# A two-part transformer kernel on one core: the second block's mixer, latent attention and tail made into one semaphore stage

## The chip, the cores and the metric

The kernel runs on one core of a Trainium2 chip. A core has five engines that run side by side, each with its own instruction queue: PE (TensorE, matrix multiply), DVE (VectorE), ACT (ScalarE), POOL (GpSimd) and SP (SyncE, which here only issues DMAs). They meet through semaphores. The metric is the device time of one execution in microseconds (us).

## The reference, cut to what matters

Two blocks of two layers each work on 512 positions of width 1024. The change is in the second block. One of its layers is

```python
u = rms_norm(x, g_mix) @ w_in
y_a = silu(layer_norm(depthwise_conv(a * sigmoid(gate))))            # conformer group
y_b = rms_norm(hgrn2(u_b), onorm) * silu(g)                           # recurrent group
y_c = gb * depthwise_conv(gc * xin)
y_d = mla(u_d)                                                        # latent attention, 4 heads
cat = rms_norm(concat(y_a, y_b, y_c, y_d) in 4 groups, g_branch)
x = x + cat @ w_out
mn = rms_norm(mem, g_mem)                                             # 256 rows of memory
q, k, v = rms_norm(rms_norm(x) @ x_wq), rms_norm(mn @ x_wk), mn @ x_wv
x = x + attention(q, k, v) @ x_wo
x = x + swiglu(rms_norm(x)) @ f_w2
```

## The kernel before

Everything is float32 and kept transposed: a tensor of width 1024 is 8 tiles of 128 partitions x 512 positions. A product with a weight tile is three float32r matmuls (`product`, L390 to L392) from a high and a low half of each operand. Weight tiles come by DMA (L358), ACT copies the high half (L367), POOL subtracts for the low half (L376).

A layer of the second block is three `nc.Block()`s, one after the other, each with one written-out instruction list per engine:

- **The mixer** (`second_mixer`): projections, the convolutions, the recurrent scan, queries and keys of the latent attention. At its end ACT takes a root for each head's key (`key_root(h)`: a Ln, L2052, then an Exp, L2054, of a sum that PE makes at L1904), squares the recurrent group (L2066) and the centred conformer group (L2073) into the buffer `PT`, and, after PE has summed those squares (L1940, L1943), takes three Ln (L2083 twice, L2085). The Exp that finishes each of these three roots is done by ACT at the start of the next block (L2337).
- **The latent attention** (`second_attention`, through `attention` and `attention_work`): 16 units (4 heads x 4 query blocks of 128). For unit n: PE scores (L743), DVE maximum and negation (L841, L844), ACT exponential (L805), DVE reciprocal (L854), POOL scaling (L880), PE transposes (L751) and ACT copies the result to `PT` (L814) four units later; after 8 units PE multiplies by the values (L757). The functions `side_act`, `side_dve`, `side_pool` put other work between the units by step number: the norm of the memory (ACT squares L529, DVE L523, L533, L540), two products that finish the conformer group (DVE L2361, steps 3 and 4), two for the recurrent group (DVE L2365, steps 5 and 6; POOL L2380, steps 8 and 10), three weight tiles. ACT and DVE follow each other closely: unit n's exponential waits for DVE's negation of n, and DVE's reciprocal of n, which stands in its list after the negation of n + 1, waits for that exponential.
- **The tail** (`second_tail`): PE sums the squares of each of the four groups of `cat` (`group_sum`, L2454), sums the memory's squares (L545), makes two key tiles of the memory (`key_tile`), then the output projection, cross attention and feed-forward.

Each of the three ends with `sem.stage_end()`, an all-engine barrier that also clears the stage's semaphores (L337):

```python
    def stage_end(self):
        numbers = sorted(s.num for s in self.numbers)
        assert numbers == list(range(numbers[0], numbers[-1] + 1))
        self.nc.all_engine_barrier(sems_to_clear=range(numbers[0], numbers[-1] + 1))
        self.stage = {}
```

The range that is cleared is that of every stage semaphore made so far: 13 at the first stage end, 76 from the second block's first mixer on. Leaving a `with nc.Block()` also writes an all-engine barrier of its own, without a clear (its rows carry the line of the `with`: L1771 for the mixer, L889 for the attention, L2438 for the tail).

Of the kernel before, what the change touches and what calls it, by code (L numbers as in the profile page):

```python
# [316 lines left out]
class Semaphores:  # L317


    def __init__(self, nc):  # L320
        self.nc, self.stream, self.stage, self.numbers = nc, {}, {}, []
# [3 lines left out]
    def __call__(self, name):  # L325
        if name in self.stream:
            return self.stream[name]
        if name not in self.stage:
            if len(self.stage) == len(self.numbers):
                self.numbers.append(self.nc.alloc_semaphore(f"stage_{len(self.numbers)}"))  # L330
            self.stage[name] = self.numbers[len(self.stage)]
        return self.stage[name]

    def stage_end(self):
# [3 lines left out]
        self.stage = {}  # L338
# [253 lines left out]
def build(nc, x_in, w1, small1, const_in, p_in, w2, small2, masks_in, mem_in, pos_in, out):  # L592
# [109 lines left out]
    def attention_work(*kinds, side_act=None, side_dve=None, side_pool=None, side_pe=None):  # L702
# [33 lines left out]
        def run_pe(pe):  # L736
            def scores(n):
                a, h, g, i = units[n]
                for m in range(a["maps"]):
                    s = first[n] + m  # L740
                    if s >= 4:
                        pe.wait_ge(sem("max_ready" if biased else "exp_done"), s - 3)
                    pe.matmul(banks[s % 4][:, 0:width(n)], a["q"](h, m, i), a["k"](h, m, width(n)), start=True,  # L743
                              stop=True).then_inc(sem("scored"), 1)

            def turn(n):
                pe.wait_ge(sem("prob_ready"), n + 1)
                if n >= 2:
                    pe.wait_ge(sem("pt_ready"), n - 1)
                for j in range(width(n) // P):  # L750
# [135 lines left out]
    def attention(weights, prefetch, work, before=None, first_act=None):  # L886

        run_pe, run_act, run_dve, run_pool = work
        with nc.Block() as block:  # L889
# [17 lines left out]
            def _(dve):  # L907
                run_dve(dve)

            @block.gpsimd  # L910
            def _(pool):
                run_pool(pool)
        sem.stage_end()
# [788 lines left out]
    B_R, DEVIATION, KEY_R = 36, 44, (45, 46, 47, 38)  # L1702
    NL = len(LEVELS)
    PAD = 15

    def second_mixer(layer, weights, prep):

        base = DEPTH * FIRST_TILES + layer * SECOND_TILES
# [62 lines left out]
        with nc.Block() as block:  # L1771
# [6 lines left out]
            def _(pe):  # L1778
# [55 lines left out]
                def scan_values(c):  # L1834
# [6 lines left out]
                    if c == 2:  # L1841
                        pe.wait_ge(sem("latent_log"), 2)
# [28 lines left out]
                pe.wait_ge(sem("kr_gained"), 1)  # L1871
# [27 lines left out]
                def key_sum(h):  # L1899
                    pe.wait_ge(sem("kr_square"), 4)  # L1900
                    pe.wait_ge(sem("key_square"), h + 1)
                    if h >= 2:
                        pe.wait_ge(sem("key_log"), h - 1)
# [874 lines left out]
```

## Time and profile before

| | |
|---|---|
| Time, median of 3 runs | 3219.67 us (3214.8 to 3219.79) |
| The profiled execution's own time | 3216.99 us |
| Its span (first to last instruction) | 3215.2 us |
| PE busy, share of the span | 95% |
| ACT / DVE / POOL busy | 41% / 50% / 49% |
| Mean granted TensorE clock | 0.984 of 2.4 GHz |

The profiled execution's time is 1.8 us more than its span. In the first layer of the second block the latent attention stands between 1903.2 and 1952.3 us of the span, in the second between 2674.2 and 2723.5. The profile names engines as above; PEld is the weight load of PE, and a `q` behind a name (ACTq) is that engine's sequencer, which runs waits, drains and barriers. PEclk is the granted TensorE clock: 1.00 is 2.4 GHz, 0.50 is 1.2 GHz.

### The profile page before, as it was taken

The page shows a single profiled execution, that of the slowest core. Times are in us where ns is not written, and L with a number is a line of the kernel's source. Part 1 is how long each engine was busy: PE and PEld are TensorE (multiplying, and loading weights), DVE is VectorE, ACT ScalarE, POOL GpSimd, SP SyncE. Part 2 cuts the span into 40 slices and gives each one's busy share as a digit, 9 for nine tenths or more (in the row PEclk, how much of TensorE's full clock was granted, in tenths as well). Part 3 has the DMA queues.
Part 4 walks back from the last instruction along what each step waited for, and adds up shares of the span by engine and source line. Part 5 has one row for each costly group of instructions (what it writes and reads, how often), then busy time and mean ns, then how long its engine had stood idle before and what let it go on. Part 6 is the DMA issues. An engine that isn't in the chain of part 4 may idle for free. (4 is left out here: it accounts for less than half of the span.)

```text
span 3215.2 us, 38320 instructions
## 1 busy us (share of the span) xinstructions
PE 3066.1 (95%) x14320; PEld 2394.0 (74%) x14320; DVE 1623.4 (50%) x2468; ACT 1327.0 (41%) x2194; POOL 1581.0 (49%) x862
## 2 busy tenths in 40 slices
PE   8989999999998999999999988899999988989999
PEld 6766788888766678888887756688888764768887
DVE  3863357732467434775348764433324955543321
ACT  4445433333443554333343475532323257442221
POOL 5634655554764455555565443344444534344443
PEclk9999999999999999999999989999999998999999
DMA  4211233333221123333323102233333211223333
GB/s 135 67 59 47 79 101 96 98 106 105 92 69 60 52 67 99 98 99 108 105 87 97 48 20 66 60 98 99 98 104 100 67 34 33 72 73 98 99 99 105
DMA packets 73736, 265.07 MB, mean 82 GB/s; under 512 B 8656, under 2 KB 9168, under 8 KB 73168
## 3 DMA queue, kind: packets, MB, share of 16 engines
q1 hardware_dynamic: 73552, 262.62, 26.6%
q8 instruction: 115, 1.88, 0.2%
q14 instruction: 69, 0.57, 0.1%
HBM read 260.49 MB, written 2.10 MB: 82 GB/s over the span
## 5 line engine op out<-in xcount | busy, mean ns | idle before, releaser
L376 POOL TENSOR_TENSOR low<-raw,high 128x1024 fp32r<-128x1024 f32 x482 | 1179.7, 2449 | 1148.8 <-ACT high L367 1115.5
L391 PE MATMUL bank<-slot_r,low 128*128 128x512 f32 (+1 forms) x3648 | 1423.8, 390 | 0.0
L392 PE MATMUL bank<-slot_r,high 128*128 128x512 f32 (+1 forms) x3648 | 1423.4, 390 | 0.0
L390 PE MATMUL bank<-slot_r,high 128*128 128x512 f32 (+1 forms) x3328 | 1323.8, 398 | 44.2 <-POOL low L376 15.0
L367 ACT ACTIVATE high<-raw 128x1024 fp32r<-128x1024 f32 x482 | 507.5, 1055 | 900.4 <-PE bank L392 826.7
L392 PEld LDWEIGHTS bank<-slot_r,high 128*128 128x128 f32 x3648 | 688.6, 189 | 147.2
L391 PEld LDWEIGHTS bank<-slot_r,low 128*128 128x128 f32 x3648 | 689.7, 189 | 144.5 <-issue 5.8
L390 PEld LDWEIGHTS bank<-slot_r,high 128*128 128x128 f32 x3328 | 629.0, 189 | 214.8 <-issue 50.3
L1624 DVE SCALAR_TENSOR_TENSOR tmp<-padded,small,tmp 128x512 f32<-128x512 f32 x176 | 209.7, 1249 | 0.0
L880 POOL TENSOR_SCALAR tmp<-tmp,stat 128x512 f32<-128x512 f32 (+3 forms) x128 | 79.9, 625 | 144.9 <-DVE stat L854 119.7
L2111 DVE SCALAR_TENSOR_TENSOR slots<-padded,small,slots 128x512 f32<-128x512 f32 x128 | 132.9, 1096 | 0.0
L1615 DVE TENSOR_TENSOR padded<-bank,rs 128x512 f32<-128x512 f32 x88 | 60.3, 686 | 138.9 <-PE bank L392 129.2
L2707 DVE TENSOR_TENSOR tmp<-bank,rs 128x512 f32<-128x512 f32 x44 | 30.4, 692 | 192.0 <-PE bank L392 186.8
L533 DVE SCALAR_TENSOR_TENSOR slot_r<-slots,small,slot_r 128x512 fp32r<-128x512 f32 (+1 forms) x80 | 93.5, 1168 | 44.0 <-ACT slot_r L520 43.7
L814 ACT ACTIVATE PT<-bank 128x256 f32<-128x256 f32 (+3 forms) x160 | 71.6, 453 | 104.8 <-PE bank L757 60.3
L743 PE MATMUL bank<-slots 64*128 64x256 f32 (+4 forms) x384 | 94.6, 501 | 18.2 <-PEq L337 15.4
L2619 ACT ACTIVATE tmp<-tmp 128x512 f32<-128x512 f32 x44 | 27.8, 632 | 203.0 <-DVE tmp L2707 203.0
L2717 DVE TENSOR_TENSOR tmp<-bank,rs 128x512 f32<-128x512 f32 x16 | 11.1, 691 | 193.1 <-PE bank L392 193.1
L751 PE MATMUL bank<-const,tmp 128*128 128x128 f32 x432 | 73.8, 294 | 36.3 <-ACT PT L814 27.6
L1367 DVE TENSOR_TENSOR slot_r<-tmp,slot_r 128x512 fp32r<-128x512 f32 x48 | 75.7, 1576 | 59.2 <-ACT slot_r L2612 59.2
L751 PEld LDWEIGHTS bank<-const,tmp 128*128 128x128 f32 x432 | 52.7, 148 | 68.2 <-issue 39.3
L390 PE MATMUL bank<-pt_r,high 128*128 128x512 f32 x256 | 101.1, 395 | 0.0
(316 smaller groups left out, 3134.4 us busy)
## 6 DMA issues: line engine op xcount, KB each, us to landing
raw<-w SPq DMA_DIRECT2D x482, 512.0 KB, 3.5
slots<-x_in SPq DMA_DIRECT2D x4, 512.0 KB, 6.5
slots<-mem_in SPq DMA_DIRECT2D x2, 1024.0 KB, 4.7
out<-slots SPq DMA_DIRECT2D x8, 256.0 KB, 4.6
const<-const_in SPq DMA_DIRECT2D x1, 1095.5 KB, 10.2
padded<-p_in SPq DMA_DIRECT2D x2, 512.0 KB, 5.1
tmp<-masks_in SPq DMA_DIRECT2D x1, 512.0 KB, 11.0
small<-small SPq DMA_DIRECT2D x2, 231.5 KB, 2.9
```

The costliest lines, as they stand in the source:

```text
L367: act.activation(self.high[:, t % PARTS, :], self.raw[:, t % RING, :], ACT.Copy).then_inc(self.sem("tile_high"), 1)
L376: pool.tensor_tensor(self.low[:, t % PARTS, :], self.raw[:, t % RING, :], self.high[:, t % PARTS, :].bitcast(F32), ALU.subtract).then_inc( ...
L390: pe.matmul(acc, lhs[0], rhs[1], start=first, stop=False)
L391: pe.matmul(acc, lhs[1], rhs[0], start=False, stop=False)
L392: return pe.matmul(acc, lhs[0], rhs[0], start=False, stop=last)
L533: dve.scalar_tensor_tensor(self.pairs[c][1], self.xs[c], self.gain[c], self.pairs[c][0].bitcast(F32), ALU.mult, ALU.subtract).then_inc(sel ...
L743: pe.matmul(banks[s % 4][:, 0:width(n)], a["q"](h, m, i), a["k"](h, m, width(n)), start=True, stop=True).then_inc(sem("scored"), 1)
L751: mm = pe.transpose(banks[4 + n % 2][:, j * P:j * P + P], prob(n)[:, j * P:j * P + P], cst("ident"))
L880: pool.tensor_scalar(prob(n), tmp[:, E + s % 4, 0:width(n)], st(3, s), 1.0, ALU.mult, ALU.mult).then_inc(sem("prob_ready"), 1)
L1367: dve.tensor_tensor(parts[g][1], tmp[:, 6 + g % 2, :], parts[g][0].bitcast(F32), ALU.subtract).then_inc(sem("hidden_low"), 1)
L1624: dve.scalar_tensor_tensor(o, padded_t[:, s % 4, 15 - tap:15 - tap + SEQ], s1("conv_w", (2 - tap) * 2 * FC + ch), o, ALU.mult, ALU.add).th ...
L2111: ins = dve.scalar_tensor_tensor(o, src, s2(w, 2 * j + c), o, ALU.mult, ALU.add)
```

## The change

Semaphores get names by part (`"mixer"`, `"latent"`, `"tail"`), so that one part can wait on those of another; the stage end behind the mixer and the one behind the latent attention are left out, in both layers. What needed them is now waited for by name (`scores_ready`, `turn_ready`, `first_act`, `first_dve`, `first_pool`). The sums and roots of the recurrent and the conformer group leave the end of the mixer and go, whole, among the units of the latent attention. In the tail the memory's sum and the first key tile stand ahead of the first two group sums. Pairs of semaphores (`key_log`, `key_rstd`) become one (`key_root`).

```diff
-        if name not in self.stage:
+        key = (part, name)
+        if key not in self.stage:
...
+    def next_part(self, part):
+        self.part = part
...
-        sem.stage_end()
+        if not joined:
+            sem.stage_end()
... in second_mixer, PE and ACT
-                for c in range(2):
-                    pe.wait_ge(sem("b_square"), c + 1)
-                    pe.matmul(banks[5 + c][:, :], cst("heads"), PT[:, 0, c, :], start=True, stop=True).then_inc(sem("b_sum"), 1)
-                for c in range(2):
-                    pe.wait_ge(sem("centered_square"), c + 1)
-                    mm = pe.matmul(banks[7][:, :], cst("ones"), PT[:, 0, 2 + c, :], start=(c == 0), stop=(c == 1))
-                mm.then_inc(sem("var_summed"), 1)
...
-                for c in range(2):
-                    act.wait_ge(sem("both"), c + 1)
-                    act.activation(PT[:, 0, c, :], S[:, Y + 2 + c, :], ACT.Square).then_inc(sem("b_square"), 1)
+                act.wait_ge(sem("both"), 2)
...
                 key_root(2)
                 key_root(3)
                 for c in range(2):
-                    act.wait_ge(sem("b_sum"), c + 1)
-                    act.activation(S[:, B_R + c, :], banks[5 + c][:, :], ACT.Ln, scale=1.0 / 64, bias=eps).then_inc(sem("b_root"), 1)
-                act.wait_ge(sem("var_summed"), 1)
-                act.activation(S[:, DEVIATION, :], banks[7][:, :], ACT.Ln, scale=1.0 / 256, bias=eps).then_inc(sem("deviation"), 1)
+                    act.activation(S[:, B_SQ + c, :], S[:, Y + 2 + c, :], ACT.Square).then_inc(sem("b_square"), 1)
+                act.wait_ge(sem("centered"), 2)
+                for c in range(2):
+                    act.activation(S[:, A_SQ + c, :], S[:, TAP_A + c, :], ACT.Square).then_inc(sem("a_square"), 1)
...
-        sem.stage_end()
... in second_attention
+        def side_pe(pe, step, place):
+            if place == "turns" and step in (2, 4):
+                c = step // 2 - 1
...
+                pe.matmul(banks[7][:, :], cst("heads"), S[:, B_SQ + c, :], start=True, stop=True).then_inc(sem("b_sum"), 1)
+            if place == "turns" and step == 6:
...
+                    mm = pe.matmul(banks[7][:, :], cst("ones"), S[:, A_SQ + c, :], start=(c == 0), stop=(c == 1))
+                mm.then_inc(sem("var_summed"), 1)
...
         def first_act(act):
-            for slot in (DEVIATION, B_R, B_R + 1):
-                act.activation(S[:, slot, :], S[:, slot, :], ACT.Exp, scale=-0.5).then_inc(sem("late_rstd"), 1)
+            act.wait_ge(mixer("query_root"), 2)
+            act.wait_ge(mixer("cos_done"), 1)
...
         def side_act(act, step):
+            if step in (3, 5):
+                c = (step - 3) // 2
+                r = S[:, B_R + c, :]
+                act.wait_ge(sem("b_sum"), c + 1)
+                act.activation(r, banks[7][:, :], ACT.Ln, scale=1.0 / 64, bias=eps).then_inc(sem("b_log"), 1)
+                act.wait_ge(sem("b_log"), c + 1)
+                act.activation(r, r, ACT.Exp, scale=-0.5).then_inc(sem("b_rstd"), 1)
+            if step == 7:
+                r = S[:, DEVIATION, :]
+                act.wait_ge(sem("var_summed"), 1)
+                act.activation(r, banks[7][:, :], ACT.Ln, scale=1.0 / 256, bias=eps).then_inc(sem("a_root"), 1)
+                act.wait_ge(sem("a_root"), 1)
+                act.activation(r, r, ACT.Exp, scale=-0.5).then_inc(sem("a_root"), 1)
...
-            if place == "end" and step in (3, 4):
-                a = S[:, TAP_A + step - 3, :]
...
+            if place == "end" and step in (6, 7):
+                c = step - 6
+                y = S[:, Y + 2 + c, :]
+                dve.wait_ge(sem("b_rstd"), c + 1)
...
+            if place == "end" and step in (8, 9):
+                a = S[:, TAP_A + step - 8, :]
+                if step == 8:
+                    dve.wait_ge(sem("a_root"), 2)
...
         def side_pool(pool, n):
-            if n in (8, 10):
-                c = (n - 8) // 2
+            if n in (10, 12):
+                c = (n - 10) // 2
...
-            if n in (12, 14):
-                weights.split_low(pool, base + n // 2 - 5)
+            if n in (11, 13):
+                weights.split_low(pool, base + (n - 9) // 2)
... in second_tail, PE
-                group_sum(0)
-                group_sum(1)
+                pe.wait_ge(latent("a_root"), 1)
+                pe.wait_ge(latent("exp_done"), 4 * NT)
+                pe.wait_ge(latent("pt_ready"), 4 * NT)
+                pe.wait_ge(latent("mem_added"), KC - 1)
+                pe.wait_ge(latent("mem_low"), KC)
                 memory.total(pe, banks[3][:, 0:MEM], cst("ones"), carried=True)
...
                 key_tile(0)
+                group_sum(0)
+                group_sum(1)
                 group_sum(2)
                 group_sum(3)
                 key_tile(1)
```

**Where the mixer meets the latent attention, on POOL.** POOL runs the barriers: the others report to it (`gather`) and it lets them go. The waits of barrier instructions are shown on the next instruction of the queue. Before, at the end of the mixer of the second block's first layer:

```order
L1771 UNCONDITIONAL_BRANCH
L337 ISA [waits barrier_Pool_Activation_PE_DVE_SP_gather]
L910 UNCONDITIONAL_BRANCH
```

And in the changed kernel, at the same place:

```order
L1787 UNCONDITIONAL_BRANCH
L921 UNCONDITIONAL_BRANCH [waits barrier_Pool_Activation_PE_DVE_SP_gather]
L889 TENSOR_SCALAR tmp<-tmp,stat 128x512 [waits stage_65,stage_87,stage_36,stage_64]
```

The clear (ISA, of `stage_end`) is gone; a wait on the barrier's `gather` semaphore, from leaving the `nc.Block()`, is still there. The same holds behind the latent attention (L898, then L2721 with the same wait), and on the other engines with `release` in place of `gather`. The last stage semaphore of the changed program is number 150, so 151 are cleared at the two stage ends of the second block that are left.

**The end of the mixer and the first units of the latent attention, on ACT.** `slots` are the working tiles, `bank` is a PSUM bank, `col` a small table. Before:

```order
L2052 ACTIVATE slots<-bank4,const 128x512 [waits stage_36]
L2054 ACTIVATE slots<-slots 128x512 [waits stage_39]
L2083 ACTIVATE slots<-bank5,const 128x512 [waits stage_42]
L2083 ACTIVATE slots<-bank6,const 128x512 [waits stage_42]
L2085 ACTIVATE slots<-bank7,const 128x512 [waits stage_44]
L1771 UNCONDITIONAL_BRANCH
L900 UNCONDITIONAL_BRANCH [waits barrier_Pool_Activation_PE_DVE_SP_release]
L2337 ACTIVATE slots<-slots 128x512 x3
L805 ACTIVATE tmp,stat<-bank0,stat,col 128x512 [waits stage_9]
```

Changed, from the same root of the last head's key to the fourth unit:

```order
L2061 ACTIVATE slots<-bank4,const 128x512 [waits stage_36]
L2063 ACTIVATE slots<-slots 128x512 [waits stage_39]
L2086 ACTIVATE slots<-slots 128x512 x2
L2089 ACTIVATE slots<-slots 128x512 [waits stage_55]
L2089 ACTIVATE slots<-slots 128x512
L1787 UNCONDITIONAL_BRANCH
L909 UNCONDITIONAL_BRANCH [waits barrier_Pool_Activation_PE_DVE_SP_release]
...
L814 ACTIVATE tmp,stat<-bank3,stat,col 128x512 [waits stage_77]
L2392 ACTIVATE slots<-bank7,const 128x512 [waits stage_68]
L2394 ACTIVATE slots<-slots 128x512 [waits stage_72]
L534 ACTIVATE slots<-slots 128x256
```

Three Ln at the mixer's end became four squares, and a Ln and an Exp now stand behind the exponentials of units 3, 5 and 7.

**The start of the tail, on PE.** The changed kernel has:

```order
L2520 UNCONDITIONAL_BRANCH [waits barrier_Pool_Activation_PE_DVE_SP_release]
L550 MATMUL bank3<-slots,const 128x256 [waits stage_80,stage_73,stage_89,stage_69,stage_81]
L2543 MATMUL bank3<-const,slots 128x1 x2
L395 MATMUL bank2<-slot_32_r_81,high 128x256 [waits tile_low]
...
L2530 MATMUL bank7<-tmp,const 128x512 [waits stage_85]
L2530 MATMUL bank7<-tmp,const 128x512
L2530 MATMUL bank6<-tmp,const 128x512 [waits stage_76,stage_85]
L2530 MATMUL bank6<-tmp,const 128x512
L2530 MATMUL bank5<-tmp,const 128x512 [waits stage_94]
```

Before, the pairs into bank7 and bank6 stood in front of the one into bank3; all four group sums now follow the first key tile. A barrier's wait still stands ahead of all of it.

## Rows read from the trace of the kernel before

**Rows 1.** The page: busy time by engine, and the last chain by engine.
```profile
PE 3066.1 (95%) x14320; PEld 2394.0 (74%) x14320; DVE 1623.4 (50%) x2468; ACT 1327.0 (41%) x2194; POOL 1581.0 (49%) x862
...
PE 13%; DVE 1%; issue 1%; ACT 1%; POOL 0%; ACTq 0%; POOLq 0%
```

**Rows 2.** One line's instructions, mixer's end: ns min/median/max, first to last start.
```profile
L1771 ACTq EVENT_SEMAPHORE  x1: 17/17/17, 1902.3 to 1902.3; - x1
...
L337 POOLq EVENT_SEMAPHORE_RANGE_CLEAR  x1: 437/437/437, 1902.6 to 1902.6; - x1
...
L337 ACTq EVENT_SEMAPHORE  x1: 17/17/17, 1903.1 to 1903.1; - x1
```

**Rows 3.** The same, behind the first layer's latent attention.
```profile
L889 ACTq EVENT_SEMAPHORE  x1: 17/17/17, 1952.5 to 1952.5; - x1
...
L337 ACTq EVENT_SEMAPHORE  x1: 17/17/17, 1953.3 to 1953.3; - x1
```

**Rows 4.** The same view, the program's first stage end (13 semaphores).
```profile
L337 POOLq EVENT_SEMAPHORE_RANGE_CLEAR  x1: 113/113/113, 26.4 to 26.4; - x1
```

**Rows 5.** Timeline, mixer's end: start us, us, engine, line, operation [idle before].
```profile
1894.31 3.63 PE L1904 MATMUL bank<-tmp,const 96*128 96x512 f32 x4
...
1895.56 1.13 ACT L2073 ACTIVATE PT<-slots 128x512 f32<-128x512 f32 x2
...
1899.48 1.25 ACT L2083 ACTIVATE slots<-bank,const 128x512 f32<-128x512 f32 x2
...
1901.44 0.69 ACT L2085 ACTIVATE slots<-bank,const 128x512 f32<-128x512 f32 x1 [0.72 <-PE bank L1943]
```

**Rows 6.** Timeline, ACT: exponentials of units 3, 6, 7, 9, 10, 11.
```profile
1909.62 0.78 ACT L805 ACTIVATE tmp<-bank,stat,col 128x512 f32<-128x512 f32 x1 [0.18 <-DVE stat L844]
...
1916.85 0.78 ACT L805 ACTIVATE tmp<-bank,stat,col 128x512 f32<-128x512 f32 x1 [0.91 <-DVE stat L844]
...
1919.42 0.78 ACT L805 ACTIVATE tmp<-bank,stat,col 128x512 f32<-128x512 f32 x1 [0.91 <-DVE stat L844]
...
1923.22 0.78 ACT L805 ACTIVATE tmp<-bank,stat,col 128x512 f32<-128x512 f32 x1 [0.24 <-DVE stat L844]
...
1925.12 0.78 ACT L805 ACTIVATE tmp<-bank,stat,col 128x512 f32<-128x512 f32 x1 [0.24 <-DVE stat L844]
...
1927.86 0.78 ACT L805 ACTIVATE tmp<-bank,stat,col 128x512 f32<-128x512 f32 x1 [0.44 <-DVE stat L844]
```

**Rows 7.** Timeline, the same stretch: POOL and DVE side by side.
```profile
1924.76 1.27 POOL L2380 TENSOR_TENSOR slots<-slots 128x512 f32<-128x512 f32 x1
...
1925.00 1.18 DVE L523 TENSOR_SCALAR slot_r<-slots,small 128x256 fp32r<-128x256 f32 x1
```

**Rows 8.** Timeline, start of the first tail.
```profile
1953.39 3.67 PE L2454 MATMUL bank<-tmp,const 128*128 128x512 f32 x8 [2.77 <-PEq L337]
...
1956.30 0.63 ACT L2557 ACTIVATE tmp<-tmp 128x512 f32<-128x512 f32 x1
...
1960.64 3.60 PE L2454 MATMUL bank<-tmp,const 128*128 128x512 f32 x8
...
1964.27 0.69 ACT L2555 ACTIVATE tmp<-bank,const 128x512 f32<-128x512 f32 x1 [0.37 <-PE bank L2454]
```

**Rows 9.** Windows: busy us and count of PE, PEld, DVE, ACT, POOL; PEclk; DMA.
```profile
1902.00:1903.00 1.00, 0.00 (x0) 0.00 (x0) 0.00 (x0) 0.13 (x1) 0.00 (x0) 1.00 0.00 0
...
1906.00:1907.00 1.00, 1.00 (x2) 0.33 (x1) 0.56 (x3) 0.65 (x3) 0.30 (x1) 0.50 1.04 442
```

**Rows 10.** Timeline, PE's weight loads for the scores, first latent attention.
```profile
1903.74 0.19 PEld L743 LDWEIGHTS bank<-slots 96*128 96x128 f32 x1 [0.24 <-issue]
1904.17 0.19 PEld L743 LDWEIGHTS bank<-slots 96*128 96x128 f32 x1 [0.24 <-issue]
...
1906.20 0.33 PEld L743 LDWEIGHTS bank<-slots 96*128 96x128 f32 x1 [0.52 <-issue]
...
1907.05 0.33 PEld L743 LDWEIGHTS bank<-slots 96*128 96x128 f32 x1 [0.52 <-issue]
```

More of the change, by code:

```diff
@@ L320, in __init__ @@
     def __init__(self, nc):
-        self.nc, self.stream, self.stage, self.numbers = nc, {}, {}, []
+        self.nc, self.stream, self.stage, self.numbers, self.part = nc, {}, {}, [], ""
         for name in ["tile_done", "tile_high", "tile_low"] + [f"tile_in_{i}" for i in range(RING)]:
@@ L325, in __call__, with of @@
     def __call__(self, name):
-        if name in self.stream:
-            return self.stream[name]
-        if name not in self.stage:
+        return self.stream[name] if name in self.stream else self.of(self.part, name)
+    def of(self, part, name):
+        key = (part, name)
+        if key not in self.stage:
             if len(self.stage) == len(self.numbers):
                 self.numbers.append(self.nc.alloc_semaphore(f"stage_{len(self.numbers)}"))
-            self.stage[name] = self.numbers[len(self.stage)]
-        return self.stage[name]
+            self.stage[key] = self.numbers[len(self.stage)]
+        return self.stage[key]
+    def next_part(self, part):
+        self.part = part
     def stage_end(self):
@@ L337, in stage_end @@
         self.nc.all_engine_barrier(sems_to_clear=range(numbers[0], numbers[-1] + 1))
-        self.stage = {}
+        self.stage, self.part = {}, ""
 class Weights:
@@ L884, in attention_work, with attention @@
         return run_pe, run_act, run_dve, run_pool
-    def attention(weights, prefetch, work, before=None, first_act=None):
+    def attention(weights, prefetch, work, before=None, first_act=None, first_dve=None, first_pool=None, joined=False):
         run_pe, run_act, run_dve, run_pool = work
@@ L1706, in second_mixer @@
     def second_mixer(layer, weights, prep):
+        sem.next_part("mixer")
         base = DEPTH * FIRST_TILES + layer * SECOND_TILES
@@ L2340, in side_act @@
             if step == 2:
                 act.wait_ge(sem("load_mem"), 16)
+                act.wait_ge(mixer("branch_c"), 2)
             if 2 <= step < 2 + KC:
@@ L2388, in second_attention, with latent @@
             query_col=lambda h, i: col[:, QUERY_R + 4 * i + h:QUERY_R + 4 * i + h + 1]),
-            side_act=side_act, side_dve=side_dve, side_pool=side_pool), before, first_act)
+            side_act=side_act, side_dve=side_dve, side_pool=side_pool, side_pe=side_pe, scores_ready=scores_ready, turn_ready=turn_ready),
+            before, first_act, first_dve, first_pool, joined=True)
     def second_tail(layer, weights, memory, lead):
+        sem.next_part("tail")
+        def latent(name):
+            return sem.of("latent", name)
         base = weights.used
@@ L2544, in _ @@
             def _(act):
+                act.wait_ge(latent("transposed"), 4 * NT)
+                act.wait_ge(sem.of("mixer", "branch_c"), 2)
+                act.wait_ge(latent("out_ready"), 4)
                 for n in range(4, KC):
```

140 lines of the change are left out of this document (90 added, 50 removed).

## The prediction

> **What bounds the kernel now.** The page comes first: PE is busy 95% of the span, no other engine more than about half of it, and the chain that ended last is mostly PE's [rows 1]. So a change elsewhere counts only where PE stands still. The mixer's end and the latent attention are such a place: between 1902 and 1903 us no engine works but ACT, for 0.13 us, and between 1906 and 1907 PE's two matmuls run at half clock while ACT and DVE work in turns [rows 9]. So I read two kinds of view next: the rows of the barriers by line [rows 2 to 4], and the timeline of the mixer's end, of the units and of the tail's start [rows 5 to 8]. There the reader is to look for the idle time in brackets. ACT waits for DVE's negation at every unit: 0.24 us where neither has side work, 0.91 where DVE has a side product [rows 6]. So the loop ACT, DVE, ACT sets the pace there: from one exponential to the next it is 1.90 us plain (1923.22 to 1925.12) and 2.57 with a product on DVE (1916.85 to 1919.42). PE and POOL follow.
>
> **The barriers.** At the mixer's end ACT is let go twice, at 1902.3 by the barrier that leaving the block writes and at 1903.1 by the stage end's, which includes a clear of 76 semaphores, 437 ns [rows 2]. Behind the latent attention it is 1952.5 and 1953.3 [rows 3]. The change takes out the second of each pair. The first stays, as its waits in the order of the changed program show, so the engines still meet. That is 0.8 us a boundary, four boundaries in two layers (I take the second layer as the first): **-3.2 us**. The cover for the new waits by name is the remaining rendezvous: all that they wait for in the part before has happened.
>
> A clear grows with its range: 113 ns for 13 [rows 4], 437 for 76 [rows 2], (437 - 113) / 63 = 5.1 ns each. The two stage ends left clear 151 in place of 76: 75 x 5.1 = 0.39 us each, **+0.8 us**.
>
> **The mixer's end.** Before, ACT starts its last three Ln at 1899.48, waits 0.72 for PE and ends at 1901.44 + 0.69 = 1902.13 [rows 5]. After, the last root of the keys is followed by four squares. That root waits for PE's fourth sum, which ends at 1894.31 + 3.63 = 1897.94 [rows 5]; with a Ln of about 0.69 and an Exp of 0.63 [rows 8] it is done by about 1899.2. Four squares at 1.13 / 2 [rows 5] are 2.26, so the end is 1901.5. That is -0.6 us a layer, **-1.2**. Both bounds: nothing, if the key's root slips to its old place and another wait follows; -1.0, if the squares slip in while ACT waits.
>
> The three Exp that leave the front of the latent attention (just over 0.6 each) are worth nothing: the first exponential of a unit waits for PE's scores and DVE's maximum, and ACT stood idle ahead of it. Without that cover, they would be 1.9 us.
>
> **Among the units.** ACT's own work for a plain unit is 1.90 - 0.24 = 1.66 us [rows 6]. A Ln and an Exp are 0.69 + 0.63 = 1.32 [rows 8], and overlap by some hundredths; I take 1.27. They exceed the idle 0.24, so the interval of such a unit is 1.66 + 1.27 = 2.93, and about 2.5 at step 3, where a small square of the memory's norm is not among the unit's work. The loop is closed: what ACT is late by, DVE's reciprocal and next negation are late by as well. DVE's products move from steps 3 to 6 to steps 6 to 9, so they and the roots stretch different units but for step 7. From unit 3 to unit 10 it was 1925.12 - 1909.62 = 15.5 us [rows 6]. After, I add seven intervals: 2.5 + 1.9 + 2.93 + 2.5 + 2.93 + 2.5 + 2.5 = 17.76, so +2.2 us. (The fifth is ACT's root at step 7; DVE's product at step 8 waits for its Exp, so nothing of it is saved.) Against it, the interval from unit 10 to 11 was 2.74, because DVE's scaling took 1.18 us beside a product of POOL [rows 7]; that product moves, and this interval should be about 2.24: -0.5. PE's sums among the units are matmuls of 3.67 / 4 = 0.9 us at full clock [rows 8], twice that at the half clock seen here [rows 9], nearly a plain unit's interval; one may hold up a score behind it, for which I put +0.3. Together +2.0 a layer, **+4.0**. Bounds: below, the roots fall in idle time and only the -0.5 stays; above, the moved product of POOL meets DVE's scaling again, +2.5.
>
> At the low bound the delay would also have to be made up later. I see nothing that could: the values of heads 0 and 1 wait for the eighth exponential's transposes, and the copies of units 8 and on follow the same list.
>
> **The tail's start.** PE's first two group sums take 3.67 us from 1953.39; the roots of groups 0 and 1 are made from about 1955.6 to 1956.9, far ahead of need [rows 8]. What ends the wait is group 3's root, a Ln at 1964.27 after PE's second pair ends at 1960.64 + 3.60 [rows 8]. Everything that PE does before that is the same work in another order, so that instant keeps its distance from the start: **0**. All four roots now come in a row, but a group's sum takes 3.67 / 2 = 1.8 us of PE and a root 0.69 + 0.63 = 1.32 of ACT [rows 8], so ACT keeps up and group 3's root waits for nothing but its own sum. If the splits of the first groups slipped behind the fourth root, one split more could stand on the path: under 1.3 us a layer, which I keep as a bound. The weights for the first key tile are split before the tail starts.
>
> **Sum.** -3.2 + 0.8 - 1.2 + 4.0 + 0 = **+0.4 us**. Against the profiled execution's 3216.99 that is 3217.4; the median of the runs shown is 3219.67, 2.7 above it, so 3220.1 beside that. Between them I say 3218. A difference under 0.2%, 6.4 us, is about what a measurement of this kernel can't tell from none.
>
> **The rivals.**
>
> *The roots are hidden (chance 0.23).* If ACT's added 1.27 us fits into its waits, as 0.91 idle beside DVE's products suggests [rows 6], the units cost nothing and the sum is -3.2 + 0.8 - 1.2 - 1.0 = -4.6: 3212.4, 3215 by the median. For it: DVE's products could overlap a root if both stood at one unit. Against it: only step 7 has both, and the plain units' idle is 0.24.
>
> *TensorE starts the latent attention at low clock (0.19).* This is the side on which it gets slower. Before, PE sums squares right up to the barrier; after, its last sum ends at 1897.94 [rows 5] and it has nothing until the scores at about 1901.9: 4 us idle in place of under two. At full clock the weight loads of the scores stand 0.43 us apart (1903.74, 1904.17), at half clock 0.85 (1906.20, 1907.05) [rows 10]; a score has two, so +0.84 each. Two scores ahead of the first exponential: +1.7 a layer, +3.4 in all, 3220.8; if two more fall low in each, +7, 3224. It decides as slower from 6.4 us in all, 3.2 a layer. Against it: the clock was low by 1906 before too, so much of this stretch is low already; and at 1902 to 1903, with PE idle, the row still reads 1.00 [rows 9].
>
> The Trainium skill, page "TensorE: Matmul & The Clock Gate", section "What's actually happening", says that the default state is the throttled one and that activity releases it. By that rule a longer idle stretch at the mixer's end speaks for this rival, and with it the time would be the rival's 3220.8; the row at 1902 agrees only as far as that idleness does not lower the clock at once.
>
> *The engines really run into each other (0.05).* With no barrier left, PE could start the scores while ACT squares, about 1.9 us more a boundary: some -8, 3209. The order of the changed program speaks against it, since each engine still waits for the barrier's release.
>
> **How the numbers follow.** The forecast has 0.53: no measurable change, its own range 3214 to 3222 (terms' bounds and the 2.7 us between profile and median). The range 3212 to 3224 takes in the hidden roots and the low clock, and leaves out the overlap and the doubled low clock. Faster by over 0.2% needs 3213.3 or less: most of the overlap, a quarter of the hidden roots and a few hundredths of the forecast: 0.13. Slower needs 3226.1 or more: a part of the low clock, and of a tail with its bound on top: 0.09. The rest is 0.78.
>
> **What the changed profile would show.** The block exits' barrier rows (L1787, L898) are there, with one release each, and the first instruction of the latent attention follows the last of the mixer by about 0.3 us in place of 1.1. The clear takes about 0.82 us. ACT's last instruction of the mixer ends some 0.6 earlier. Between the exponentials of units 3 and 10 there are 17.8 us, not 15.5, and ACT's idle time ahead of those behind a root is gone. The tail's group 3 root keeps its distance of 10.9 us from PE's first instruction. I am wrong if the units keep their pace, if PE's clock reads 0.50 from the first score on, or if an engine waits by name for something in the part before.

## The result, and the profile after

| | before | changed |
|---|---|---|
| Median of 20 runs each | 3215.63 us | 3222.72 us |
| Profiled execution's span | 3215.2 us | 3216.9 us |
| Mean granted TensorE clock | 0.984 | 0.983 |

The changed kernel is slower: its ratio to the kernel before is 1.002, 95% interval 1.0013 to 1.0026, so 4.2 to 8.4 us. (One of its 20 runs took 7587.9 us and is left out of the ratio.) Over 20 runs the median of before is 4 us lower than over the three runs that the prediction had, so the comparison is the ratio and not 3218 against 3222.72.

The two profiled spans differ by 1.7 us only, because the changed execution was 2.1 us ahead when the second block's first mixer began (1678.4 us against 1680.5). From there on it is 1538.5 us against 1534.7, so 3.8 more. That is less than the 6.4 us of the ratio: the profiled changed execution, 3218.72 us, is 4 us below the median of its kernel. Where its other executions lose the rest is not shown. The reader should compare stretches. From the second block's first mixer on, by the release of the barriers:

| Stretch | before, layer 1 / 2 | changed, layer 1 / 2 |
|---|---|---|
| mixer, to the block exit's release | 221.8 / 222.2 us | 218.1 / 220.9 |
| second barrier and clear behind it | 0.8 / 0.8 | none |
| latent attention, to its block exit's release | 49.4 / 49.6 | 54.2 / 53.8 |
| second barrier and clear behind it | 0.8 / 0.8 | none |
| tail, to its block exit's release | 497.0 / 489.9 | 497.4 / 491.7 |
| stage end behind it | 0.8 / 0.8 | 1.2 / 1.2 |

The latent attention takes 4.8 and 4.2 us more. In the first layer the mixer, the barriers and the rest give nearly all of it back (+0.3 us in all), in the second they do not (+3.5).

The barriers first, by line, in the changed kernel. They answer to [rows 2]:

```profile
L1787 PEldq DRAIN  x1: 2107/2107/2107, 1890.5 to 1890.5; - x1
L1787 ACTq DRAIN  x1: 2729/2729/2729, 1893.6 to 1893.6; - x1
...
L1787 ACTq EVENT_SEMAPHORE  x1: 17/17/17, 1896.5 to 1896.5; - x1
...
L342 POOLq EVENT_SEMAPHORE_RANGE_CLEAR  x1: 847/847/847, 2448.3 to 2448.3; - x1
```

One release at the mixer's end in place of two, no clear there, and the clear of 151 semaphores is 847 ns long at the stage end that stays. Then TensorE's clock in windows of 2 us around the mixer's end (busy us of PE, PEld, DVE, ACT, POOL, then the granted clock), for [rows 9]:

```profile
1891.00:1893.00 2.00, 1.52 (x4) 0.38 (x2) 1.94 (x3) 1.54 (x4) 1.38 (x1) 0.82 0.00 0
1893.00:1895.00 2.00, 0.00 (x0) 0.00 (x0) 1.94 (x3) 1.97 (x4) 1.93 (x2) 0.50 0.00 0
1895.00:1897.00 2.00, 0.13 (x1) 0.16 (x1) 0.96 (x2) 1.30 (x3) 0.99 (x1) 0.50 0.00 0
1897.00:1899.00 2.00, 2.00 (x3) 0.97 (x4) 0.00 (x0) 0.00 (x0) 0.00 (x0) 0.50 0.70 172
1899.00:1901.00 2.00, 2.00 (x3) 0.72 (x3) 1.25 (x3) 0.87 (x2) 0.00 (x0) 0.50 0.83 352
```

The same place in the kernel before, some six us later on its scale, which was not among the rows ahead of the prediction:

```profile
1895.00:1897.00 2.00, 2.00 (x4) 0.79 (x3) 1.94 (x3) 1.95 (x5) 1.26 (x1) 0.50 0.00 0
1897.00:1899.00 2.00, 2.00 (x5) 0.86 (x4) 1.93 (x3) 1.94 (x5) 0.59 (x1) 0.78 0.00 0
1899.00:1901.00 2.00, 2.00 (x6) 0.76 (x4) 0.86 (x2) 1.72 (x3) 1.92 (x2) 1.00 0.00 0
1901.00:1903.00 2.00, 0.41 (x1) 0.00 (x0) 0.00 (x0) 0.69 (x1) 0.00 (x0) 1.00 0.00 0
```

In both kernels the clock falls to 0.50 (1.2 GHz) around the last key sums: in windows of 0.5 us at about 1894.5 in the kernel before, as they begin, and at about 1892.3 in the changed kernel, as they end. In the kernel before TensorE goes from the key sums straight to the sums of the squares, at 1897.73, and the clock is back at 1.00 (2.4 GHz) from about 1897.9 on, so with the first of them; in the second layer it is back 1.0 us after they begin. It is still 1.00 when the scores begin. In the changed kernel the sums of the squares are gone from there, TensorE stands idle for 4.35 us, and the clock stays at 0.50 under the scores until about 1902.5. TensorE's first scores, before and changed:

```profile
1903.24 7.08 PE L743 MATMUL bank<-slots 96*128 96x512 f32 x12 [1.83 <-PEq L337]
```

```profile
1896.87 5.46 PE L750 MATMUL bank<-slots 96*128 96x512 f32 x6 [4.35 <-PEq L1787]
```

The timeline of ScalarE shows what follows, from the last square over the first exponentials; it answers to [rows 5, 6]:

```profile
1895.17 1.13 ACT L2089 ACTIVATE slots<-slots 128x512 f32<-128x512 f32 x2
1900.08 0.78 ACT L814 ACTIVATE tmp<-bank,stat,col 128x512 f32<-128x512 f32 x1 [3.78 <-DVE stat L853]
...
1904.42 0.77 ACT L814 ACTIVATE tmp<-bank,stat,col 128x512 f32<-128x512 f32 x1
...
1905.17 0.68 ACT L2392 ACTIVATE slots<-bank,const 128x512 f32<-128x512 f32 x1
1905.88 0.63 ACT L2394 ACTIVATE slots<-slots 128x512 f32<-128x512 f32 x1
...
1913.98 0.78 ACT L814 ACTIVATE tmp<-bank,stat,col 128x512 f32<-128x512 f32 x1 [0.91 <-DVE stat L853]
...
1922.23 0.78 ACT L814 ACTIVATE tmp<-bank,stat,col 128x512 f32<-128x512 f32 x1 [0.84 <-DVE stat L853]
...
1924.42 0.78 ACT L814 ACTIVATE tmp<-bank,stat,col 128x512 f32<-128x512 f32 x1
```

From the release to the first exponential it is 3.6 us (1896.5 to 1900.08); before it was 2.2 (1903.1 to 1905.35). Units 3 to 10 take 1922.23 - 1904.42 = 17.8 us, unit 10 to 11 takes 2.19, units 11 to 15 take 13.57 where it was 11.91 before. The last of these is mostly the values. The values of the first two heads, PE's long matmul group, took 5.29 us in the changed kernel's first layer (from 1926.49) and 3.65 in the same place before (from 1929.92); in the second layer it was 3.67 after and 5.35 before. The tail's first squares and group 3's root, for [rows 8]:

```profile
1950.86 2.19 ACT L2630 ACTIVATE tmp<-slots 128x512 f32<-128x512 f32 x4 [0.36 <-PEq L898]
...
1961.96 0.69 ACT L2639 ACTIVATE tmp<-bank,const 128x512 f32<-128x512 f32 x1 [0.37 <-PE bank L2530]
```

They stand 11.1 us apart; before, 10.9. In the second layer it is 12.6 against 10.9. The first layer of the latent attention is accounted for by these rows: +1.3 us to the first exponential, +0.1 in units 0 to 3, +2.3 in units 3 to 10, -0.5 from unit 10 to 11, +1.7 in units 11 to 15, in all 4.8.

### The profile page after: what moved, and what is told of

It is laid out like the page before. It is cut to its first block and busy times, and to the rows that moved or that the text cites. A ratio compares the mean times of both kernels' runs of the same rounds, so it can differ in the third digit from the quotient of the medians.

```text
span 3216.9 us, 38316 instructions
## 1 busy us (share of the span) xinstructions
PE 3064.2 (95%) x14320; PEld 2393.0 (74%) x14320; DVE 1625.6 (51%) x2468; ACT 1327.0 (41%) x2194; POOL 1583.0 (49%) x862
## 5 line engine op out<-in xcount | busy, mean ns | idle before, releaser
L2801 DVE TENSOR_TENSOR tmp<-bank,rs 128x512 f32<-128x512 f32 x16 | 11.1, 691 | 193.1 <-PE bank L397 193.1
```

## The experiments

Each was timed in the same sessions as the kernel before; ratios are to it. "The changed kernel" is 1.0020 in these terms.

### e1: TensorE gets other work at the mixer's end

```diff
                 pe.wait_ge(sem("v_evac"), 2)
+                for _ in range(4):
+                    pe.matmul(banks[5][:, :], cst("ones")[0:96, :], tmp[0:96, K_SQ + 3, :], start=True, stop=True)
                 pe.sem_inc(sem("tile_done"), 2)
```

> The changed kernel with four extra matmuls behind the mixer's last key sum on TensorE (their result is never read), where the four that the change took away stood; everything else as changed. Theory A (TensorE's clock falls because the sums left the mixer's end): the granted clock at the first scores returns to what it was before, the first exponential follows the barrier's release in about 2.2 us in place of 3.6, and the time falls by 1.3 to 3 us a layer: ratio to the kernel before 1.0005 to 1.0012. Theory B (the roots among the units are the whole cost, the clock is chance): nothing changes, ratio 1.0020.

3216.22 us, ratio 1.0008 (0.9999 to 1.0017): work that nobody needs takes some 4 us off the changed kernel by the ratios. The two intervals still touch (the changed kernel's begins at 1.0013), so the time alone would be thin evidence; the trace shows where it comes from. Windows, TensorE's first scores and ScalarE's timeline of this run:

```profile
1897.00:1899.00 2.00, 2.00 (x6) 0.76 (x4) 0.78 (x2) 2.00 (x5) 1.27 (x1) 1.00 0.00 0
1899.00:1901.00 2.00, 1.44 (x4) 0.58 (x4) 0.00 (x0) 0.15 (x1) 0.00 (x0) 1.00 0.30 41
```

```profile
1899.97 3.67 PE L750 MATMUL bank<-slots 96*128 96x512 f32 x8 [0.56 <-PEq L1787]
```

```profile
1902.23 0.78 ACT L814 ACTIVATE tmp<-bank,stat,col 128x512 f32<-128x512 f32 x1 [3.08 <-DVE stat L853]
...
1905.24 0.76 ACT L814 ACTIVATE tmp<-bank,stat,col 128x512 f32<-128x512 f32 x1
```

The clock is 1.00 again at the first scores. The first score starts at 1899.97, so the first exponential follows in 2.26 us (changed: 1896.87 to 1900.08, 3.21), and units 0 to 3 take 3.01 us (changed: 4.34 in the first layer, 4.81 in the second). That is 2.3 and 2.8 us a layer. Theory A holds for the start of the latent attention; B, by which nothing would change, doesn't. Units 3 to 10 stay at 17.8 and 17.4 us.

### e2: sums, roots and products back at their old places

The edit in words, against the changed kernel:

- In the mixer TensorE again sums the squares (four sums, into banks 5, 6 and 7), and ScalarE again squares into `PT` and takes three Ln at the end.
- In the latent attention ScalarE again takes the three Exp first, VectorE's products stand in steps 3 to 6, GpSimd's in 8 and 10.
- `side_pe` and the three roots in `side_act` are gone.

> The changed kernel with the sums, roots and products of the recurrent and conformer group put back where they were before (end of the mixer, start of the latent attention); the stage ends stay out and the tail keeps its new order. Theory A and B: all of the loss goes, and the barriers' gain stays, 3.2 - 0.8 = 2.4 us: ratio 0.9992. Theory C (the waits by name or the tail's new order cost): the loss stays at least in part, ratio 1.001 or more.

3216.61 us, ratio 1.0004 (0.9995 to 1.0013). Most of the loss goes, as expected, but 0.9992 is below the interval: the barriers' 2.4 us are not to be seen. The profile shows one place where they can have gone. In its second layer TensorE finished the latent attention's last values early and then stood idle for long. The same values in the first layer, then the timeline of PE and the windows at the second layer's tail:

```profile
1944.77 5.50 PE L766 MATMUL bank<-PT,slots 128*64 128x512 f32 x16 [0.69 <-ACT PT L823]
```

```profile
2713.64 3.65 PE L766 MATMUL bank<-PT,slots 128*64 128x512 f32 x16 [0.69 <-ACT PT L823]
2721.57 1.19 PE L550 MATMUL bank<-slots,const 128*128 128x256 f32 x2 [4.28 <-PEq L898]
```

```profile
2720.00:2722.00 2.00, 0.42 (x1) 0.46 (x2) 0.00 (x0) 1.61 (x4) 0.62 (x1) 0.50 0.00 0
2722.00:2724.00 2.00, 2.00 (x9) 1.82 (x9) 0.00 (x0) 1.57 (x4) 1.73 (x1) 0.50 0.85 225
```

The second layer's tail then started at half clock, and from its first squares to group 3's root it was 13.5 us, where it was 11.1 in the first layer: 2.4 us lost. Finishing the values 1.85 us sooner gave nothing back, as TensorE began the tail 7.93 us after their start in both layers. One execution shows this; that it is what most of them do is not shown.

### e3: the barriers at the block exits really gone

```diff
+        with nc.Block() as shared[0]:
             second_mixer(layer, weights, lead)
             memory = memory_prep()
             second_attention(layer, weights, memory)
...
             second_tail(layer, weights, memory, lead)
         sem.stage_end()
... in each of the three (in attention() for the latent attention alone)
-        with nc.Block() as block:
+        with contextlib.nullcontext(shared[0]) as block:
```

> The changed kernel with mixer, latent attention and tail of a layer written into one nc.Block(), so that the barriers at the block exits between them really are gone and only the waits by name are left. If engines can run ahead: TensorE starts the scores some 4 us before the squares end on ScalarE, and ScalarE's first exponential then waits only for its own list: about 3.5 us a layer at this place; behind the latent attention TensorE starts the memory's sum and the first key tile while ScalarE ends its squares, up to 3 us a layer. In all 8 to 13 us less than the changed kernel: ratio to the kernel before 0.998 to 0.9995. Rival (the rendezvous costs nothing because the chain goes through ScalarE anyway): within 2 us of the changed kernel, ratio 1.0015 to 1.002.

3208.56 us, ratio 0.9976 (0.9968 to 0.9985): 14 us less than the changed kernel, 7 less than the kernel before, a little more than expected. PE and ACT at the mixer's end, then PE and ACT at the tail's start:

```profile
1892.03 3.55 PE L1923 MATMUL bank<-tmp,const 96*128 96x512 f32 x4
1896.07 4.61 PE L753 MATMUL bank<-slots 96*128 96x512 f32 x5 [0.48 <-DVE slots L2252]
```

```profile
1897.91 1.13 ACT L2092 ACTIVATE slots<-slots 128x512 f32<-128x512 f32 x2
1899.28 0.78 ACT L817 ACTIVATE tmp<-bank,stat,col 128x512 f32<-128x512 f32 x1 [0.23 <-DVE stat L856]
```

```profile
1941.67 6.22 PE L769 MATMUL bank<-PT,slots 128*64 128x512 f32 x16 [0.69 <-ACT PT L826]
1947.82 0.70 PE L551 MATMUL bank<-slots,const 128*128 128x256 f32 x2
```

```profile
1949.27 2.19 ACT L2633 ACTIVATE tmp<-slots 128x512 f32<-128x512 f32 x4
```

TensorE starts the scores while ScalarE still makes the key's roots and the squares, and ScalarE waits 0.23 us for its first exponential where it waited 3.78. At the tail TensorE has begun the memory's sum before ScalarE's first square. But the clock at the first scores was still low: from 1896 to 1902 it read 0.50, and units 0 to 3 took 4.7 us in both layers. TensorE had been idle for 0.48 us only, and the clock had been at 0.50 since about 1892.3, while it was busy with the key sums. So the changed kernel's long standstill is not needed to make the scores slow. What e3 has in common with it is that the sums no longer stand between the key sums and the scores. Whether a break as short as 0.48 us matters too is not shown. The tails took 9.5 us from the first squares to group 3's root, and neither started at half clock, so part of the 14 us may be the clock at the tails.

### e4: the tail's old order

```diff
+                group_sum(0)
+                group_sum(1)
                 memory.total(pe, banks[3][:, 0:MEM], cst("ones"), carried=True)
...
                 key_tile(0)
-                group_sum(0)
-                group_sum(1)
```

> The changed kernel with the tail's old order on TensorE: group sums 0 and 1, then the memory's sum and the first key tile. By the prediction's step the order is worth nothing: ratio 1.0020, as the changed kernel. If the second layer's later tail start in the changed trace (1.7 us) comes from the order, 1.0010 to 1.0015.

3222.87 us, ratio 1.0029 (1.0018 to 1.0040): no gain from the old order, so the new order costs nothing that can be seen. Its profile is of the slowest of its seven executions (3229.18 us). Both tails in it started at half clock (13.9 and 12.9 us from the first squares to group 3's root), so a late start as in the changed kernel's second layer comes with the old order too.

### e5: three Ln among the units, Exp and products late

```diff
             if step in (3, 5):
...
                 act.activation(r, banks[7][:, :], ACT.Ln, scale=1.0 / 64, bias=eps).then_inc(sem("b_log"), 1)
-                act.wait_ge(sem("b_log"), c + 1)
-                act.activation(r, r, ACT.Exp, scale=-0.5).then_inc(sem("b_rstd"), 1)
+            if step == 11:
... (the three Exp; the one of step 7 goes there too)
... (DVE: products in steps 12 to 15, not 6 to 9;  POOL: after units 14 and 15, not 10 and 12)
```

> The changed kernel with only the three Ln left behind units 3, 5 and 7; the three Exp stand together behind unit 11, where ScalarE waits for TensorE's values, and what needs them follows: VectorE's four products in steps 12 to 15, GpSimd's two in 14 and 15. If the stretching of the units is the sum of side work as the prediction has it, units 3 to 10 take 1.66 + 0.69 = 2.35 at three places and 1.90 at four, 14.7 us in place of 17.8, and the kernel gains 2 to 3 us a layer on the changed one: ratio to the kernel before 1.0000 to 1.0008. Rival (the time is only moved, given back at the values or in the second half): ratio 1.0020. TensorE's clock at the first scores stays low, 3.2 us from first score to first exponential.

3211.73 us, ratio 0.9989 (0.9980 to 0.9998): 10 us less than the changed kernel, more than expected. ScalarE's units 3, 4, 10 and 11, the three Exp, and the wait for the values:

```profile
1907.35 0.78 ACT L814 ACTIVATE tmp<-bank,stat,col 128x512 f32<-128x512 f32 x1 [0.24 <-DVE stat L853]
...
1909.06 0.78 ACT L814 ACTIVATE tmp<-bank,stat,col 128x512 f32<-128x512 f32 x1
...
1920.94 0.78 ACT L814 ACTIVATE tmp<-bank,stat,col 128x512 f32<-128x512 f32 x1 [0.24 <-DVE stat L853]
...
1923.13 0.78 ACT L814 ACTIVATE tmp<-bank,stat,col 128x512 f32<-128x512 f32 x1
...
1924.37 1.16 ACT L2397 ACTIVATE slots<-slots 128x512 f32<-128x512 f32 x2
1925.41 0.64 ACT L2400 ACTIVATE slots<-slots 128x512 f32<-128x512 f32 x1
...
1928.95 0.60 ACT L823 ACTIVATE PT<-bank 128x512 f32<-128x512 f32 x1 [2.15 <-PE bank L766]
```

Units 3 to 10 take 1920.94 - 1907.35 = 13.6 us, 4.2 less than in the changed kernel (3.8 in the second layer); a unit with a Ln takes 2.12, not 2.35. The Exp stand where ScalarE waited anyway: it still waits 2.15 us for the values behind them. Nothing is given back later. On the contrary, units 11 to 15 take 11.9 us in both layers, where the changed kernel took 13.6 and 12.8, and with the units 3 to 10, which were expected to save 3.1 us, that is why the gain is more than expected. The first exponential again came 3.2 us after the first score.

### e6: one block and the late order together

> One block for the three parts, as e3, with the order of e5. If both gains are independent: 4 to 6 us less than e3, ratio 0.9958 to 0.9965. Rival as in e5: 0.9976 as e3.

3198.59 us, ratio 0.9950 (0.9937 to 0.9962), 16 us below the kernel before: the fastest of all that ran. Its page:

```profile
span 3195.6 us, 38272 instructions
...
PE 3056.5 (96%) x14320; PEld 2388.5 (75%) x14320; DVE 1635.7 (51%) x2468; ACT 1325.7 (41%) x2194; POOL 1579.9 (49%) x862
```

By the medians it is 10 us below e3 and 13 below e5 (8 and 13 by the ratios), so the two gains do not eat each other. Against e7 below, in which the sums stand at their old places, it is 7 us by the ratios: moved late, the roots do gain something.

### e7: one block, sums at their old places

> One block for the three parts with sums, roots and products where they were before (as e2). It tells whether moving the sums is worth anything once nothing meets at a barrier: TensorE's scores stand behind the sums again and start near 1901.5 on the scale of the kernel before, 1.8 us earlier than there, at full clock; the tail's start gains 1.6 us as in e3. 3.4 us a layer, minus 0.4 for the clear: ratio 0.9981, close to e3. If moving the sums was what lets the engines overlap, 0.999 or more.

3207.04 us, ratio 0.9972 (0.9961 to 0.9983), against 0.9976 (0.9968 to 0.9985) of e3: the intervals overlap. Moving the sums, the way the change did, shows no gain once the barriers are gone. What it gains ahead of the scores it loses again: among the units 3 to 10, e3 took 17.8 and 17.4 us, e7 15.3. TensorE's scores stand right behind the sums, at full clock, and ScalarE's first exponential follows the three Exp with no wait:

```profile
1899.21 1.88 PE L1962 MATMUL bank<-PT,const 128*128 128x512 f32 x4
1900.92 5.46 PE L753 MATMUL bank<-slots 96*128 96x512 f32 x12
```

```profile
1901.93 1.67 ACT L2380 ACTIVATE slots<-slots 128x512 f32<-128x512 f32 x3
1903.50 0.76 ACT L817 ACTIVATE tmp<-bank,stat,col 128x512 f32<-128x512 f32 x1
```

### e8: the four stage ends five times over

```diff
-        self.nc.all_engine_barrier(sems_to_clear=range(numbers[0], numbers[-1] + 1))
+        for _ in range(times):
+            self.nc.all_engine_barrier(sems_to_clear=range(numbers[0], numbers[-1] + 1))
... (times is 5 behind the mixer and behind the latent attention, in both layers)
```

> The kernel before with each of the four stage ends that the change leaves out written five times over (barrier and clear of 76). If one costs 0.8 us as read from the rows, 16 more cost 12.8 us: ratio 1.0040. If a longer standstill also lowers TensorE's clock behind it, 2 to 3 us more at each of four places: ratio 1.0065 or more.

3234.21 us, ratio 1.0061 (1.0047 to 1.0074), 20 us more. ScalarE's wait at the mixer's end and the windows there:

```profile
1904.61 1.67 ACT L2338 ACTIVATE slots<-slots 128x512 f32<-128x512 f32 x3 [4.30 <-PEq L338]
...
1907.69 0.78 ACT L806 ACTIVATE tmp<-bank,stat,col 128x512 f32<-128x512 f32 x1 [1.41 <-DVE stat L845]
```

```profile
1900.00:1902.00 2.00, 0.00 (x0) 0.00 (x0) 0.00 (x0) 0.31 (x1) 0.00 (x0) 1.00 0.00 0
1902.00:1904.00 2.00, 0.00 (x0) 0.00 (x0) 0.00 (x0) 0.00 (x0) 0.00 (x0) 0.81 0.00 0
1904.00:1906.00 2.00, 1.37 (x2) 0.83 (x3) 0.00 (x0) 1.39 (x3) 0.00 (x0) 0.50 0.34 49
```

The wait grew from 1.08 to 4.30 us: 3.22 for four barriers, 0.805 each, which is the 0.8 of the prediction, and 12.9 us for sixteen. The other 7 us are the clock, as far as the profile shows: here TensorE did nothing from 1899.6 on, the clock fell during that, at about 1903.2, and the first exponential came 3.06 us after the first score instead of 2.1. Most of it is at the tails: both started at half clock, 13.8 us from the first squares to group 3's root instead of 10.9.

### e9: late order, with e1's unread matmuls

> The order of e5 (Exp and products late) with the four unread matmuls of e1 at the mixer's end, barriers at the block exits kept. If clock and stretching are two separate terms, the first score is followed by the first exponential in 2.3 us in place of 3.2, units 0 to 3 take 3.0 us in place of 4.6, and 2 to 3 us a layer come on top of e5: ratio 0.9972 to 0.9980 (e5 had 0.9989). If they are one effect, 0.9989.

3208.60 us, ratio 0.9976 (0.9967 to 0.9985), against 0.9989 (0.9980 to 0.9998) of e5: 4 us, as in e1, and again the intervals touch. First score to first exponential 2.26 us, units 0 to 3 3.01 us, units 3 to 10 13.5 us, in both layers. The clock at the first scores and the stretching are two terms, and each can be taken out alone.

## Why the prediction was wrong

**The step that failed** is the one that priced TensorE's missing work at nothing. The forecast took the start of the latent attention as unchanged and left the clock to a rival with a chance of 0.19; its argument was that "the clock was low by 1906 before too, so much of this stretch is low already". It was low in part: the kernel before had a first exponential 2.1 us after its first score in both layers, and units 0 to 3 in 4.3 and 3.0 us. In the changed kernel it is 3.2 us, and 4.3 and 4.8. Taking it out gives 2.3 to 2.8 us a layer in e1's trace, and some 4 us in all by its ratio and again by e9's.

The rival had 1.7 us a layer. It was right that the scores would run at low clock, but it put the cause in 4 us of idleness. The rows show the clock already at half when the key sums end (at about 1892.3, the last of them until 1892.5), and e3, with 0.48 us of idleness, has it low as well. What the kernel before had was work behind the key sums without a break. In every run that has it (before, e1, e2, e7, e8, e9) the first layer's clock was back at 1.00 between 0.1 and 2.4 us after that work began, and, but for e8 with its long standstill, the first exponential came 2.1 to 2.6 us after the first score. In every run that lacks it (the changed kernel, e3, e4, e5, e6) it came after 3.21 us, in both layers. By the page "TensorE: Matmul & The Clock Gate" of the Trainium skill, section "What's actually happening", activity is what releases the throttle: the traces agree with that, as the clock of the kernel before and of e1 went from 0.50 to 1.00 while TensorE worked without a break.

**The units**: right where the forecast looked. 17.76 us forecast from unit 3 to 10, 17.81 and 17.38 measured; 2.24 from 10 to 11, 2.19 and 2.20 measured. The +0.3 for a sum at half clock was not needed. So the term is 1.5 to 1.8 us a layer, and not the 2.0. The close hit from 3 to 10 has some luck in it: the intervals behind a root took 2.31, 2.81 and 2.82 us (forecast 2.5, 2.93, 2.93), and the one from unit 8 to 9 made up for it in the first layer with 2.93 (forecast 2.5). At step 3 the small square is among the unit's work after all; what is missing there is the copy to `PT`.

Behind unit 11 the forecast had no term, and there was one. Units 11 to 15 took 12.6 to 13.6 us in all eight layers that have the whole roots among the units (the changed kernel, e1, e3, e4). In the other fourteen they took 11.9 us, but for two at 13.5 and 13.6. In the eight, TensorE's granted clock was 0.50 for some us during the values of heads 0 and 1, during the scores and transposes just ahead of them, or during both. That is 0.7 to 1.7 us a layer; e5, which moves only the Exp and what follows them, is rid of it.

**The barriers**: the price was right, 0.8 us each (e8: 0.805), and the second release is gone; the clear cost 847 - 437 = 410 ns more against 390 forecast. Between ScalarE's last square and TensorE's first score there were 0.57 us and not 0.3; before, from ScalarE's last Ln to its next instruction, 1.08. But e2 shows that the price of a wait isn't the gain of removing it: its 2.4 us did not appear in the time (1.0004, at best 0.9995, against 0.9992). This is a second miss of the sum, and its cause is open. That both block exits still hold the engines together was right, and e3 shows what it hid: 14 us.

**The mixer's end**: 0.6 us a layer forecast. From the Ln of the last key root to ScalarE's last instruction it was 1902.13 - 1898.24 = 3.89 us before and 1896.30 - 1892.89 = 3.41 after, so 0.5. The whole mixer gave 1.3 in the second layer; that this is because the squares no longer stand ahead of the key roots is argued, not shown. The first layer gave 3.7, of which some 3 us are no gain of the change: in that execution of the kernel before, the last key sums ran at half clock (3.63 us against 2.02), and so did matmuls near 1865 (a mean clock of 0.84 over 10 us against 1.00).

**The tail**: right that the order is worth nothing (e4). One reading was off, without consequence: 1955.6 to 1956.9 us is the root of group 0 alone, that of group 1 followed from 1957.1 to 1958.5. That tails can start at half clock, at 1.5 to 3.0 us each, was in no term. It was so in eight of the sixteen tails that begin behind a barrier, and in none of the six of the one-block runs. The eight follow what TensorE did before. Leaving out e8 with its longer standstill, all eight tails behind last values of 5.2 to 5.8 us took 10.9 to 11.1 us from first squares to group 3's root; the three behind values of 3.65 us (wholly at full clock, with some 4.3 us of idleness after them) took 13.5 to 13.9; the three behind values of 6.4 to 6.5 us took 12.6 to 12.9. What sets the length of the values in turn is open.

**The sum.** The forecast had +0.4 us, the ratio says +6.4 (4.2 to 8.4). The clock at the first scores is some 4 us of that by e1, and 2.4 us of gain from the barriers did not come by e2. The moved work apart from the clock cost less than its term: from e2 to e1 it is 1 us where the forecast had 4.0 - 1.2 = 2.8. These differences are uncertain by 3 to 4 us each, so they show which terms were off but not by how much. The range in absolute time held 3222.72 only by luck, because the three runs of before that it leaned on were on the slow side of their kernel's spread: 1.0020 times their 3219.67 would have been 3226.1, outside it.

**What stays open**: what decides in which executions the values and the tail find the clock high, where e2's 2.4 us went in most executions, and what the executions of the changed kernel without a profile, 4 us slower in the median than the one shown, do differently.

## What to carry to other kernels

Work that is taken off TensorE may have kept up the clock of what follows. Where a chain of small matmuls stands behind it, each of which another engine waits for, look at the granted clock row by row, and ask what TensorE did when it came back up. Find out from the instruction order whether a barrier is really gone, since a block's exit writes one of its own; waits by name paid here only when nothing else made the engines meet (e2: no gain to be seen; e3 against the changed kernel: 14 us). And side work in a closed loop of two engines, where each waits for the other, stretched the units that it stood in; a better place for it was where an engine waited for a third (e5: 10 us for the same instructions).

## What the runs showed of the hardware

- TensorE's granted clock can fall while PE is busy all the time: between 1892 and 1897 us of the kernel before PE was busy in every microsecond, until 1894.4 with 4-column matmuls, and the clock went from 1.00 to 0.50 at about 1894.5. It was back at 1.00 at about 1897.9, when PE had worked without a break on 512-column matmuls, first the last key sums, at half clock.
- Four matmuls with no reader made a program faster by some 4 us (e1: 1.0008 against 1.0020; again e9: 0.9976 against 0.9989).
- An all-engine barrier with a clear of 76 semaphores costs 0.805 us of standstill (e8); the clear is 113 ns for 13 semaphores, 437 for 76 and 847 for 151, some 5.3 ns for each more. Sixteen of them cost 20 us and not 13; in the profile the clock fell from 1.00 to 0.50 in the long standstill, at about 1903.2 with TensorE idle since 1899.6, and both tails started at half clock.
